# Unread matmuls in four places of TensorE's order, an early square root, and a modulation row copied ahead of the samples' x

## What is computed

```python
mod = silu(c) @ w_ada + b_ada                       # 9 rows of c, 6 * 1024 columns
sh_mix, sc_mix, gt_mix, sh_ffn, sc_ffn, gt_ffn = split(mod, 6)
h = rmsnorm(x, g_pre_mix) * (1 + sc_mix) + sh_mix
u, qkv, z, a, b = split(h @ w_in)
pool_out = pool_mixer(u); q, k, v = silu(causal_conv(qkv))
o, s_new = gated_delta_rule(q, k, v, g(a), beta(b), s0)
mix = concat(pool_out, norm(o) * silu(z)) @ w_out
x = x + gt_mix * rmsnorm(mix, g_post_mix)
h = rmsnorm(x, g_pre_ffn) * (1 + sc_ffn) + sh_ffn
f = moe_ffn(h)                                      # top 4 of 32 experts, clamped SwiGLU
x = x + gt_ffn * rmsnorm(f, g_post_ffn)
```

## Time and profile before

| | |
|---|---|
| three runs | 1192.16 us median (1191.81 to 1194.58) |
| the profiled execution | 1194.63 us, its span 1192.8 us |
| TensorE busy | 1023.1 us, 86% |
| VectorE / ScalarE / GpSimd busy | 399.4 / 172.6 / 122.6 us |
| DMA | 463.66 MB, 389 GB/s on the mean |
| the chain that ended last | TensorE 67%, DMA 18%, VectorE 6% |

### The profile page before, as it was taken

The page is one execution under the profiler, slowest core; times in us unless marked ns, Lnnn a source line. Parts: engine busy times, 40 slices in busy tenths (PEclk is TensorE's granted clock), DMA queues, the critical chain, the costliest instruction groups (busy, mean ns, idle before and its releaser), DMA issues.

```text
span 1192.8 us, 31868 instructions
## 1 busy us (share of the span) xinstructions
PE 1023.1 (86%) x11942; PEld 494.6 (41%) x11943; DVE 399.4 (33%) x1163; ACT 172.6 (14%) x467; POOL 122.6 (10%) x323
## 2 busy tenths in 40 slices
PE   5999999988898788997689998998866899999864
PEld 4778777544333224332233244333322333333421
DVE  2145594875223123231122232332111223332313
ACT  3241314252000001000000010000000000001102
POOL 0150102101001001010000110010100000010100
PEclk9998999989999899999899999999878999999997
DMA  9985937999999999999999997999999999999996
GB/s 324 316 306 208 355 95 222 391 347 412 426 427 429 430 425 429 430 430 425 430 430 426 428 427 305 429 427 430 429 427 429 430 429 426 429 429 430 426 429 279
DMA packets 78230, 463.66 MB, mean 389 GB/s; under 512 B 11803, under 2 KB 31585, under 8 KB 53546
## 3 DMA queue, kind: packets, MB, share of 16 engines
q1 hardware_dynamic: 73055, 461.56, 94.3%
q10 hardware_dynamic: 5139, 1.60, 0.6%
HBM read 455.56 MB, written 7.57 MB: 388 GB/s over the span
## 4 chain that ended last, share of the span: by engine, by line
PE 67%; DMA 18%; DVE 6%; issue 4%; SPq 3%; DVEq 1%; ACT 1%; ACTq 0%
PE psum L678 26%; PE psum L697 14%; DMA weights<-in_w_gu 12%; PE psum L1065 6%; PE psum L653 4%; DMA work<-in_w_down 4%; PE psum L630 2%; PE psum L1028 2%; SPq L963 2%; PE psum L647 2%; PE psum L1352 2%; DMA weights<-in_w_ada 2%; PE psum L1069 2%; DVE work L2455 1%; DVE work L2460 1%
## 5 line engine op out<-in xcount | busy, mean ns | idle before, releaser
L678 PE MATMUL psum<-weights,work 128*32 128x512 f32 x2928 | 346.7, 613 | 91.6 <-DMA weights<-in_w_gu 45.9
L678 PEld LDWEIGHTS psum<-weights,work 128*32 128x32 f32 x2928 | 92.7, 111 | 311.5 <-issue 240.1
L697 PE MATMUL psum<-weights,work 128*32 128x256 f32 x2624 | 167.1, 407 | 33.6 <-DVE work L2469 31.3
L2455 DVE STREAM_TRANSPOSE work<-psum 128x256 f32<-128x256 f32 x53 | 23.9, 450 | 419.7 <-PE psum L678 416.9
L697 PEld LDWEIGHTS psum<-weights,work 128*32 128x32 f32 x2624 | 86.4, 116 | 108.4 <-issue 63.7
L1870 ACT ACTIVATE work<-work x53 | 22.1, 416 | 503.3 <-DVE work L2459 483.8
L630 PE MATMUL psum<-work 128*32 128x257 f32 (+1 forms) x1296 | 90.4, 393 | 3.2 <-ACT work L1867 3.2
L2479 DVE STREAM_TRANSPOSE work<-work 128x288 f32<-128x288 f32 x53 | 25.3, 478 | 195.0 <-PE psum L653 195.0
L1065 PE MATMUL psum<-work,weights 128*128 128x288 f32 x320 | 82.1, 413 | 0.0
L630 PEld LDWEIGHTS psum<-work 128*32 128x32 f32 (+1 forms) x1296 | 38.4, 111 | 70.4 <-issue 62.2
L1065 PEld LDWEIGHTS psum<-work,weights 128*128 128x128 f32 x320 | 60.2, 192 | 17.8 <-issue 2.0
(11 more groups left out here) (405 smaller groups left out, 912.5 us busy)
## 6 DMA issues: line engine op xcount, KB each, us to landing
weights<-in_w_gu SPq DMA_DIRECT2D x112, 2048.0 KB, 35.8
weights<-in_w_down SPq DMA_DIRECT2D x48, 2048.0 KB, 38.8
work<-in_w_gu SPq DMA_DIRECT2D x16, 2048.0 KB, 35.9
work<-in_w_down SPq DMA_DIRECT2D x16, 2048.0 KB, 42.0
weights<-in_w_ada SPq DMA_DIRECT2D x12, 2048.0 KB, 10.1
weights<-in_w_in SPq DMA_DIRECT2D x5, 2048.0 KB, 12.9
weights<-in_w_out SPq DMA_DIRECT2D x2, 2048.0 KB, 9.8
out<-weights SPq DMA_DIRECT2D x12, 256.0 KB, 4.2
```

The costliest lines, as they stand in the source:

```text
L678: last = mm(bank(GB)[SLOTS * n:SLOTS * n + SLOTS, :].rearrange("p (a x) -> p a x", a=4), xTm[:, k, :], gu[:, k % 2, n], start=k == 0, stop ...
L697: last = mm(bank(YB)[SLOTS * q:SLOTS * q + SLOTS, 0:QW], hT[:, k, :], dn[:, k % 4, QW * q:QW * q + QW], start=k == 0, stop=k == KT - 1)
L2455: v.transpose(features, of_slots[0]).then_inc(s["hid_step"], 1)
```

## The change

Nothing that reaches an output is computed otherwise. A helper `keep_warm(b, n)` issues n matmuls of the identity matrix with four copies of itself (128 x 512 values) into PSUM bank b, which nobody reads. It is called in four places: behind the transposes of c (4 matmuls), behind the setup transposes (4), behind the first two `ada_T` (3), and behind the transposes of the first and third chunk in the router (5). ScalarE issues the five small vectors ahead of the two states. It takes one root of one value right behind silu. VectorE copies the result of `ada(0)` ahead of the samples' x.

```diff
@@ TensorE
+            def keep_warm(b, n):
+
+                for _ in range(n):
+                    mm(bank(b), ident, ident.unsqueeze(1).to_broadcast([P, 4, P]), start=True, stop=True)
+
...
             last.then_inc(s["setup_ps"], 1)
+            keep_warm(7, 4)
             pe.wait_ge(s["rows_in"], 16 * (N_VEC + N_HIST))
...
+            keep_warm(7, 4)
             pe.wait_ge(s["setup_sb"], 1)
             ada(0)
...
+            keep_warm(2, 3)
             pe.wait_ge(s["hT_s"], 1)
             half_unit(0, 0)
             half_unit(1, 0)
...
             transposes_x2(0, 6)
             transposes_x2(1, 1)
+            keep_warm(0, 5)
             logit_parts(0, 6, 7)
             transposes_x2(2, 4)
@@ ScalarE
-            act.dma_start(hist_rows[0:24, :], state_conv[0].rearrange("b t c -> (b t) c")).then_inc(s["rows_in"], 16)
-            act.dma_start(phist_rows[0:120, :], state_pool[0].rearrange("b t c -> (b t) c")).then_inc(s["rows_in"], 16)
-
...
             act.dma_start(v2[0:72, :], conv_w.rearrange("a j (r n) -> (a j r) n", n=P)).then_inc(s["rows_in"], 16)
+            act.dma_start(hist_rows[0:24, :], state_conv[0].rearrange("b t c -> (b t) c")).then_inc(s["rows_in"], 16)
+            act.dma_start(phist_rows[0:120, :], state_pool[0].rearrange("b t c -> (b t) c")).then_inc(s["rows_in"], 16)
+
             act.wait_ge(s["c_in"], 48)
             fn(c_sb[0:SEQS, :], c_sb[0:SEQS, :], ACT.Silu).then_inc(s["c_silu"], 1)
+            act.wait_ge(s["stats_set"], 1)
+            fn(st[0:1, 14:15], st[0:1, 13:14], ACT.Sqrt)
...
             act.wait_ge(s["x_in"], 32)
-            act.wait_ge(s["stats_set"], 1)
@@ VectorE
-            v.wait_ge(s["xT_ps"], KT // 2 + 1)
-            v.tensor_copy(hT[:, :, SEQ:TOK], bank(3)[:, 256:512].rearrange("p (k t) -> p k t", k=KT)).then_inc(s["hT_s"], 1)
             for half in range(2):
                 ks = slice(KT // 2 * half, KT // 2 * (half + 1))
                 for t in range(2):
                     i = half + 2 * t
                     v.wait_ge(s["slot_used"], used("ada", i))
                     v.tensor_copy(mraw[:, i], ada_out(i)).then_inc(s["mod_sb"], 1)
+                    if i == 0:
+                        v.wait_ge(s["xT_ps"], KT // 2 + 1)
+                        v.tensor_copy(hT[:, :, SEQ:TOK], bank(3)[:, 256:512].rearrange("p (k t) -> p k t", k=KT)
+                                      ).then_inc(s["hT_s"], 1)
```

## The result

The changed kernel takes **1198.46 us** (median of 9 runs, 1193.96 to 1202.59) against 1192.16 (9 runs of the kernel before, 1189.32 to 1194.79). The ratio is **1.0054, 95% interval 1.0040 to 1.0069**: slower by half a per cent. The forecast was 1191.4, range 1188.6 to 1194.4. It was wrong, and in its sign. One execution of a later run (`e19`, 1258.84 us at a mean granted clock of 0.835, where the others have 0.96) is of a slower kind and is left out of that run's ratio.

A forecast was written before the change was run, and what follows sets the result against it. The kernel's end was taken as bound by the DMA weight stream, its restart by TensorE's path before 250 us. The opening's 2.1 us, credited at 0.8 against the median 1192.16, gave 1191.4 us, range 1188.6 to 1194.4.

The forecast's parts named there:

- The opening: TensorE's work up to the third `ada`: first `ada` 2.0 us later, half units done at 31.7 against 33.83, 2.1 us won.
- Fill 1: Four matmuls behind the transposes of c, starting at 7.13 us and ending at 13.0, depending on when the clock rises.
- fill 3: Three matmuls before the first half units: 2.65 us where the wait was 1.41, ending at 28.0.
- the bound of 2.6: The third `ada`'s data lands at 31.2 us, so the opening can win no more than 2.6 us.
- The rule against it: Transposes don't count as clock activity: the clock could drop behind the setup transposes, 1.4 us lost in place of 2.1 won.
- Fill 2: Four matmuls behind the setup transposes, at full clock 3.5 us, ending at 18.2; no wait there that it could shorten.
- Fill 4 worth nothing: Five router matmuls from 257.07 to 261.5 us; first expert 0.4 later to 1.3 earlier, hidden by the busy DMA stream.
- A microsecond won before 250 us moves the stream's restart and the end by a microsecond: Claim that gains before the weight loads resume (245.25 us before) reach the kernel's end in full; later ones are taken back.
- 0.8 of the opening's 2.1: Gain credited against the median of 1192.16 us, since a median run may lack the slow clock stretch at 28.9 us.
- The rivals: "All of it shows", opening and router gains giving 1188.3 us, chance 0.10; and "Nothing shows", 1192.2 us, chance 0.25.
- the one on the slower side: Clock drops behind the setup transposes, second fill 3.5 us longer, 1.4 us lost; an outcome told as slower got 0.05.
- Nothing shows: Transfers in the opening take back TensorE's gain, or the second fill and a missing slow stretch cancel it: 1192.2 us, chance 0.25.

The follow-up runs named there:

- e19: e1 plus one alignment directive at the start of TensorE's program, moving the code behind it about 64 instructions further on, no added products; ratio 1.0018 [1.0004, 1.0033].
- e7: The changed kernel with the moving side of all 16 fill products cut from 512 values to one; ratio to the kernel before 1.0040 [1.0024, 1.0057].
- e3: The kernel before plus only the five fill products in the router; ratio 1.0002 [0.9983, 1.0020].
- e1: The change without its four fills, keeping the reordered loads, early root and earlier modulation copy; ratio to the kernel before 0.9997 [0.9982, 1.0012], median 1192.63 us.
- e16: e1 plus 32 products one value wide behind TensorE's first wait; ratio to the kernel before 1.0061 [1.0041, 1.0081].
- e12: e1 plus 48 products one value wide behind TensorE's first wait; ratio to the kernel before 1.0127 [1.0094, 1.0161].
- e9: The kernel before, in its own order, plus 16 products one value wide behind TensorE's first wait; ratio 1.0037 [1.0019, 1.0056].
- e15: e1 plus 16 one-value products behind TensorE's first wait, with 16 products taken out of the modulation's eleventh part at 134.9 us; ratio 1.0021 [1.0001, 1.0040].
- e18: The change with all fills, the second half of the small level-update products moved behind the next unit; ratio to the kernel before 1.0039 [1.0021, 1.0058].
- e4: The changed kernel run again, unaltered; ratio to the kernel before 1.0050 [1.0030, 1.0069].
- e5: The change with only its first two fills (8 products) and the reordering; ratio to the kernel before 1.0017 [1.0000, 1.0034].
- e6: The change with only its third fill (3 products) and the reordering; ratio to the kernel before 0.9999 [0.9987, 1.0010].
- e17: e1 with the second half of the small level-update products moved behind the next unit; ratio to the kernel before 1.0005 [0.9984, 1.0026].
- e2: The change without the five fill products in the router; ratio to the kernel before 1.0034 [1.0017, 1.0052].

## Why the prediction was wrong

- **The opening** was right, its gain a little too low: 2.7 us where 2.1 was forecast. Fill 1 ended at 12.7 (forecast 13.0), the setup transposes at 14.4 (14.6), the first `ada` began at 17.76 (18.2), the second at 22.16 without a wait (22.7), fill 3 ended at 27.4 (28.0). The third `ada` was at 31.11 (31.7), just past the bound of 2.6 that its tile sets. In `e7` TensorE waits 1.46 us for that tile, so the bound itself was right.
- **The rule against it**, that transposes don't count as activity for the clock (the Trainium skill, TensorE: Matmul & The Clock Gate, Part 4), changed nothing here. Fill 2 ran at the full clock right behind 22 setup transposes: 3.61 us for 8 records, as the earlier trace rows give for 16 in 7.13. The 1.9 us of transposes in between did not bring it down. That is no test of the rule over a longer stretch. In `e7`, where they followed 2.39 us of standing, they and most of the first `ada` (3.28 us) were slow.
- **Fill 4 worth nothing** was right: `e3` gives 1.0002, and the clock stayed at 1.00 from 257 to 268.
- **"A microsecond won before 250 us moves the stream's restart and the end by a microsecond"** is right in its second half and not shown in its first. From the restart to the end it is 947.6 to 950.7 us in all 20 traces. But a gain in the opening need not reach the restart: with the third `ada` between 30.9 and 31.6 us it lies anywhere from 239.2 to 246.1. At the median, `e1` with its third `ada` 2.3 us earlier is the same within −2.1 and +1.4 us. I had credited 0.8 of the opening's 2.1, which the interval allows. `e16` and `e12` delay the third `ada` by 6.1 and 10.0 us and are 7.9 and 15.8 us above `e1`'s median, but the cost of their added products is in that as well.
- **The step that failed is one that the sum never had.** Each fill was priced by its time on TensorE and by who waits for it, and where a wait covered it, at nothing. Without the fills the loss is gone (`e1` 0.9997, the change 1.0054). `e7` and `e9` show that their time on the path is not what costs: products that hold nothing up cost 0.4%. A term for what added fills do elsewhere was put at nothing, without a reason. It measured some 4 to 6 us for 11 to 16 products, against a forecast gain of 0.8 at the median and 2.1 in the trace. The traces show a piece of it, the 1.7 to 2.5 us at the eleventh `ada` in the four kernels with three full fills. The path from the opening to the restart was taken as TensorE's alone, and in those four traces it ran over the transfer of `l_blocks` and VectorE. What the rest of the term is made of stays open.
- **The rivals** all turned on the clock or on transfers, and the one on the slower side was priced for a mechanism that did not occur (the fills at the lower clock). "Nothing shows" is what `e1` does, the change without its fills.
- **The width** was at fault too. The range built on three runs of the kernel before, 2.8 us apart. Nine of them lie 5.5 us apart, and the 29 beside `e9` lie 11.4. The change's nine lie 8.6 apart, so it isn't the change that spreads them.

**What stays open.** Settled is that 11 to 16 products added to TensorE's program in the opening cost 0.3 to 0.5%, also where they hold nothing up, and that as many behind the mixer cost nothing that can be measured. Where between the opening and the router the time goes, and by what mechanism, is open. The code's place may have a share (`e19`), and `e15` says that its place behind 135 us is perhaps not all. The late `l_blocks` transfer is a part of it in four traces, and no run tests it. The starved place behind 184 us is ruled out as the cause of the loss (`e18`). In six of the nine kernels with 11 or more added ahead, the profiled execution was the fastest of its own set (the change, `e4`, `e7`, `e9`, `e12`, `e16`), so most traces lack what the others lost, and the starved place costs them less than it costs `e5` or `e6`. `e18`'s trace is typical. It starts the eleventh `ada` at 138.9 us, `e17` at 135.8. So it is 3.4 us behind ahead of the starved place, and 1.0 behind it, since it stands there 0.47 us against 1.81 and keeps its clock. At the end it is 1.4 behind. No version tried beats the kernel before: the best is `e1`, at 0.9997 [0.9982, 1.0012].

## What to carry to other kernels

Filler work that hides in a wait was not free in this long unrolled program. Test it first with fillers of the same number and as little length as possible, in idle time, and read in the trace that they fit into it: here a product one value wide still took 0.43 us. If that is slower, tuning the length is not enough. Where an opening becomes faster, look at the small transfers that other engines wait for later on, and not only at the large ones. When a change of some microseconds in the trace doesn't reach the median, compare the profiled execution with the spans of the other runs before explaining the trace: it may be the fastest one, which doesn't hold the loss. And look for idle time with no releaser ("issue") that stays at one record number while the code around it changes. In this case that engine was waiting for its instructions.

## What the runs showed of the hardware

- TensorE can run out of instructions. It did in 19 of the 20 traces (17 times at record 1729, in `e12` one transfer further on, in `e19` where the shift put it; not in `e16`), 0.5 to 2.6 us, in most of them behind small products whose records start 8 to 16 ns apart. The instruction transfer that landed in the gap (16 KB, by `e12` 256 instructions) took 0.9 to 1.6 us, and TensorE went on 1.3 to 1.6 us behind its end.
- Standing that long can bring the clock down behind it: 0.50 for 6.8 us after 2.63 us, not after 0.87; after 2.24 us in one trace not, after 2.25 in another yes. After 1.81 (`e17`) and 1.85 us (`e2`) it was 0.50 for 3.4 us.
- A product of an identity matrix with a moving side mostly of zeros holds the clock up: 8 records in 3.61 us. With one moving value, a product of 128 rows and columns still took 0.43 us (96 records of 48 products in 20.64 us), and about 0.24 us where the clock was full (6 records in 0.73 us in `e7`).
- A small transfer beside the stream of weight tiles took 7.7 to 15.3 us from issue to landing (`l_blocks`, 20 traces), and its landing decided when TensorE went on in four of them.
